# Attention on one core: the product of probabilities and values as three rounded products, one item later

## The reference, cut to what matters

```python
def one_block(qi):
    s = jnp.einsum('bqhd,bkhd->bhqk', qi, k).astype(jnp.float32) * sm_scale
    p = jax.nn.softmax(s, axis=-1).astype(v.dtype)
    return jnp.einsum('bhqk,bkhd->bqhd', p, v)
```

## Time and profile before

| | us |
|---|---|
| three runs | 4581.32, 4586.82, 4589.06 |
| median | 4586.82 |
| span of the profiled execution | 4584.7 |
| first layer's attention, items (from 583.6 us) | 7 heads at about 56.3 each, then the last |
| second layer's attention, items (from 1557.0 us) | 7 heads at about 53.1 each, then the last |

### The profile page before, as it was taken

One profiled execution on the slowest core, in us unless ns is written; L12 is line 12 of the kernel. 1 busy time (PEld: TensorE's weight loads), 2 busy tenths in 40 slices (PEclk: granted clock), 3 DMA queues, 4 the chain that ended last, 5 costly groups with the idle time before them and its releaser, 6 DMA issues. The chain is left out here.

```text
span 4584.7 us, 42478 instructions
## 1 busy us (share of the span) xinstructions
PE 3953.7 (86%) x16276; PEld 2819.4 (61%) x16276; DVE 2099.5 (46%) x2655; ACT 1550.5 (34%) x2451; POOL 673.8 (15%) x332
## 2 busy tenths in 40 slices
PE   4799799999798799996857899889999855999996
PEld 1687455568586355583636666567777744666664
DVE  0391466651372566622356423233442213666665
ACT  1412345550422445413141335222220012555542
POOL 0221200002221100020101010123333222011111
PEclk9899899999899799987988899999999966999997
DMA  4211100111210121222312110233333234999975
GB/s 165 74 37 30 35 19 29 32 42 65 78 47 26 42 66 56 65 83 53 40 40 52 45 21 10 42 75 83 88 86 68 74 112 129 359 352 358 353 290 213
DMA packets 346632, 451.05 MB, mean 98 GB/s; under 512 B 51965, under 2 KB 221106, under 8 KB 344898
## 3 DMA queue, kind: packets, MB, share of 16 engines
q1 hardware_dynamic: 331186, 405.28, 29.3%
q0 software_dynamic: 12656, 25.26, 1.5%
q10 hardware_dynamic: 2592, 17.83, 1.0%
HBM read 408.39 MB, written 59.31 MB: 102 GB/s over the span
## 5 line engine op out<-in xcount | busy, mean ns | idle before, releaser
L1144 PE MATMUL values<-probs,vp 128*128 128x512 f32 x672 | 348.6, 600 | 12.0 <-issue 6.4
L1232 ACT ACTIVATE probs<-scores 128x512 f32<-128x512 f32 (+1 forms) x336 | 196.0, 583 | 306.3 <-PE scores L219 304.6
L217 PE MATMUL scores<-q_hi,k_rest 97*128 97x512 f32 (+1 forms) x336 | 262.3, 781 | 0.0
L3382 PE MATMUL dp<-h_t,abt 128*128 128x512 f32 x544 | 241.9, 598 | 1.1 <-ACT abt L3431 0.9
L261 POOL TENSOR_TENSOR ring_r<-ring_w,ring_hi 128x1024 fp32r<-128x1024 f32 x44 | 136.8, 3111 | 702.5 <-ACT ring_hi L254 702.5
L3413 ACT ACTIVATE expert_hi<-wu 128x1024 fp32r<-128x1024 f32 x136 | 144.8, 1065 | 251.4 <-PE gp L219 251.4
L1313 DVE TENSOR_REDUCE mx<-made 128x1 f32<-128x640 f32 (+1 forms) x272 | 203.9, 794 | 27.2 <-PE made L1085 26.4
L217 PE MATMUL smb<-x_t_r,merge_w_r 128*128 128x512 f32 x480 | 196.1, 408 | 22.2 <-POOL merge_w_r L2723 19.4
L217 PE MATMUL gates_ps<-x_t_r,ring_r 128*128 128x512 f32 (+1 forms) x560 | 206.5, 369 | 2.5 <-PEq L83 2.5
L734 DVE SCALAR_TENSOR_TENSOR conv_out<-conv_in,vectors,conv_out 128x1295 f32<-128x1295 f32 (+1 forms) x120 | 205.9, 1716 | 4.3
L218 PE MATMUL gates_ps<-h_t_r,ring_hi 128*128 128x512 f32 (+1 forms) x560 | 206.4, 369 | 0.0
(11 more groups left out here) (527 smaller groups left out, 9504.9 us busy)
## 6 DMA issues: line engine op xcount, KB each, us to landing
wg<-in_w_gate SPq DMA_DIRECT2D x34, 2048.0 KB, 9.8
wu<-in_w_up SPq DMA_DIRECT2D x34, 2048.0 KB, 11.0
h_t<-in_w_down SPq DMA_DIRECT2D x34, 2048.0 KB, 9.9
ahead_w<-in_w_ada SPq DMA_DIRECT2D x48, 512.0 KB, 3.9
ring_w<-in_w_in SPq DMA_DIRECT2D x44, 512.0 KB, 4.0
mod_w<-in_w_mod ACTq DMA_DIRECT2D x8, 1536.0 KB, 29.1
ahead_w<-in_w_mod SPq DMA_DIRECT2D x24, 512.0 KB, 3.5
out_w<-in_w_out SPq DMA_DIRECT2D x24, 512.0 KB, 5.2
```

What stands on the lines that cost most here:

```text
L217: nc.tensor.matmul(out, lhs[1], rhs[0], start=start, stop=False, **kw)
L1144: nc.tensor.matmul(O[b % 2][:, 0:w], vp[g // 2 % 2][:, kb, g % 2 * VD:g % 2 * VD + P], pr[m % 3][:, 0:w], start=kb == 0, stop=kb == nk - 1 ...
L1232: nc.scalar.activation(pr[m % 3][:, 0:w], S[m % 2][:, 0:w], ACT.Exp, scale=scale).then_inc(s.exped, 1)
L3382: m = nc.tensor.matmul(dp[half][:, :], at[:, j, :], wd[u][:, j, half * 512:(half + 1) * 512], start=j == 0, stop=j == FK - 1)
```

## The change

- The value product becomes a split product of three: values and probabilities are each split into a rounded part and a rest (`v_hi`, `v_rest`; `probs_hi`, `probs_rest`).
- The probabilities of an item are rounded by ScalarE, except for the items of steps `first_k + 1` to `NB + 1` (steps 3 to 7 in the first layer, 3 to 6 in the second), which VectorE rounds. In step n it is item n+1 that is rounded, ahead of everything else in the step. GpSimd subtracts to get the rest, 336 times.
- The value product of an item is issued one step later than before.
- Value tiles: the even head's values have one place, the odd head's two; VectorE makes their rests, three instructions for two heads.
- The row of maxima and the identity in `turn_max` are float32 instead of the rounded format.
- Smaller: three tiles (`o`, `turned`, `krope`) are given up and others used in their place; the transfers for `add_ahead` have one buffer instead of two, and the six steps are others (6, 10, 13, 17, 19, 21 in place of 9, 11, 13, 17, 19, 21 in the first layer; 5, 9, 12, 15, 17, 19 in place of 8, 10, 12, 15, 17, 19 in the second). GpSimd sets constants in two instructions over all value tiles, with a tensor as input, where it had four memsets.

```diff
--- before.py
+++ after.py
@@ -956,7 +956,12 @@
...
-    ahead_slots = (first_piece + 1, first_piece + 3, first_piece + 5, NI - 5, NI - 3, NI - 1)
+    ahead_slots = (first_piece - 2, first_piece + 2, first_piece + 5, NI - 5, NI - 3, NI - 1)
+    total = NI * HEADS
+    by_act = [not first_k + 1 <= (m - 1) % NI <= NB + 1 for m in range(total)]
+    rounded_before = [sum(by_act[:m]) for m in range(total)]
@@ -977,37 +982,52 @@
...
+    pr_rest = [at_x(f"probs_rest{i}", 512, 32 * D + 2 * D * i, F32R) for i in range(3)]
+    pr_hi = [at_x(f"probs_hi{i}", 512, 28 * D + 2 * D * i, F32R) for i in (0, 1, 5)]
...
-        vp = [sb(f"vp{i}", [P, NT, 3 * VD]) for i in range(2)]
+        vh, vr = (sb(n, [P, NT, 5, VD], F32R) for n in ("v_hi", "v_rest"))
...
-        mx_r, ident_r = sb("mx_r", [P, NT], F32R), sb("ident_r", [P, P], F32R)
+        mx_r = sb("mx_r", [P, NT])
...
+        def item(m):
+            qb, kb = items[m % NI]
+            t0, w, nk = q_blocks[qb]
+            return m // NI, qb, kb, t0, w, nk
+
+        def wait_rounded(eng, m):
+            if by_act[m]:
+                eng.wait_ge(s.p_hi_act, rounded_before[m] + 1)
+            else:
+                eng.wait_ge(s.p_hi_dve, m - rounded_before[m] + 1)
@@ -1037,8 +1057,14 @@
...
-            for i in range(2):
-                once(nc.gpsimd.memset(vp[i][:, :, VD:2 * VD], 1.0))
+            ones = k.ones[:, 0:2 * VD].rearrange("p (a d) -> p a d", d=VD).unsqueeze(1).broadcast_to([P, NT, 2, VD])
+            for values, constant in ((vh, 1.0), (vr, 0.0)):
+                once(nc.gpsimd.tensor_scalar(values[:, :, 1:4:2, :], ones, constant, None, ALU.mult))
+            for m in range(total):
+                w = item(m)[4]
+                wait_rounded(pool, m)
+                nc.gpsimd.tensor_tensor(pr_rest[m % 3][:, 0:w], pr[m % 3][:, 0:w], pr_hi[m % 3][:, 0:w].bitcast(F32),
+                                        ALU.subtract).then_inc(s.p_rest, 1)
@@ -1049,7 +1075,7 @@
...
-                    pe.wait_ge(s.v_kept, 3 * ((g - 1) // 2 + 1))
+                    pe.wait_ge(s.v_rest, 3 * ((g - 1) // 2 + 1))
@@ -1088,10 +1114,8 @@
...
-                if g == 0:
-                    pe.wait_ge(s.ident_made, 1)
...
-                    m = nc.tensor.matmul(J[0:1, j // 4, (j % 4) * P:(j % 4 + 1) * P], mx_r[:, j:j + 1], ident_r[:, :],
+                    m = nc.tensor.matmul(J[0:1, j // 4, (j % 4) * P:(j % 4 + 1) * P], mx_r[:, j:j + 1], k.ident,
@@ -1132,20 +1156,24 @@
...
-            def weigh(g, n):
-                qb, kb = items[n]
-                _, w, nk = q_blocks[qb]
-                m, b = NI * g + n, NQ * g + qb
-                if n == 0:
-                    pe.wait_ge(s.v_kept, 3 * (g // 2 + 1))
+            def weigh(m):
+                g, qb, kb, _, w, nk = item(m)
+                b, e = NQ * g + qb, g % 2
+                if m % NI == 0:
+                    pe.wait_ge(s.v_rest, 3 * (g // 2 + 1))
...
-                pe.wait_ge(s.exped, m + 1)
-                nc.tensor.matmul(O[b % 2][:, 0:w], vp[g // 2 % 2][:, kb, g % 2 * VD:g % 2 * VD + P], pr[m % 3][:, 0:w],
-                                 start=kb == 0, stop=kb == nk - 1).then_inc(s.weighed, 1)
+                first = 1 + 2 * (g // 2 % 2) if e else 0
+                V, V_rest = [x[:, kb, first:first + 2, :].rearrange("p a d -> p (a d)") for x in (vh, vr)]
+                wait_rounded(pe, m)
+                nc.tensor.matmul(O[b % 2][:, 0:w], V, pr_hi[m % 3][:, 0:w], start=kb == 0, stop=False)
+                nc.tensor.matmul(O[b % 2][:, 0:w], V_rest, pr_hi[m % 3][:, 0:w], start=False, stop=False)
+                pe.wait_ge(s.p_rest, m + 1)
+                nc.tensor.matmul(O[b % 2][:, 0:w], V, pr_rest[m % 3][:, 0:w], start=False, stop=kb == nk - 1)\
+                    .then_inc(s.weighed, 1)
@@ -1156,13 +1184,15 @@
...
-                    weigh(g, n)
+                    if g or n:
+                        weigh(NI * g + n - 1)
...
+            weigh(total - 1)
@@ -1205,9 +1235,9 @@
...
-                if p >= 2:
-                    act.wait_ge(s.weighed, 2 * (p - 1) * NI)
-                dst = vp[p % 2][:, 4 * n:4 * n + m, :].rearrange("p j (a d) -> p j a d", d=VD)[:, :, 0:3:2, :]
+                if p:
+                    act.wait_ge(s.weighed, (2 * p - 1) * NI)
+                dst = of_pair(vh, p)[:, 4 * n:4 * n + m, :, :]
@@ -1231,20 +1261,26 @@
...
+            def round_weights(m):
+                w = item(m)[4]
+                act.wait_ge(s.exped, m + 1)
+                if m >= 3:
+                    act.wait_ge(s.weighed, m - 2)
+                nc.scalar.activation(pr_hi[m % 3][:, 0:w], pr[m % 3][:, 0:w], ACT.Copy).then_inc(s.p_hi_act, 1)
...
-                    act.wait_ge(s.divided, b)
+                    act.wait_ge(s.gated, b)
...
-            nc.scalar.activation(ident_r[:, :], k.ident, ACT.Copy).then_inc(s.ident_made, 1)
@@ -1252,8 +1288,12 @@
...
+            round_weights(0)
...
+                    m = NI * g + n + 1
+                    if m < total and by_act[m]:
+                        round_weights(m)
@@ -1311,6 +1351,21 @@
...
+            def rest_of_values(p, n):
+                m = min(4, NT - 4 * n)
+                dve.wait_ge(s.v_kept, 3 * p + n + 1)
+                hi_part = of_pair(vh, p)[:, 4 * n:4 * n + m, :, :].bitcast(F32)
+                dst = of_pair(vr, p)[:, 4 * n:4 * n + m, :, :]
+                src = J[:, v_banks[n], 0:m * P].rearrange("p (j a d) -> p j a d", j=m, d=VD)
+                nc.vector.tensor_tensor(dst, src, hi_part, ALU.subtract).then_inc(s.v_rest, 1)
+            def round_weights(m):
+                w = item(m)[4]
+                dve.wait_ge(s.exped, m + 1)
+                if m >= 3:
+                    dve.wait_ge(s.weighed, m - 2)
+                nc.vector.tensor_copy(pr_hi[m % 3][:, 0:w], pr[m % 3][:, 0:w]).then_inc(s.p_hi_dve, 1)
@@ -1328,16 +1383,16 @@
...
+                if g % 2 == 0 and n >= NI - 3:
+                    rest_of_values(g // 2, n - (NI - 3))
@@ -1379,6 +1434,9 @@
...
+                    m = NI * g + n + 1
+                    if m < total and not by_act[m]:
+                        round_weights(m)
...
```

55 lines of the change are left out of this document (27 added, 28 removed).

## The result

The changed kernel takes 4692.0 us in the median of 4 runs (4688.4 to 4700.0), the kernel before 4586.9 beside it (4581.3 to 4589.1). The ratio is 1.0233, with a 95% interval of 1.0219 to 1.0248. The forecast was 4644 with a range of 4568 to 4700. So the sign and the place were right, but the loss is 105 us and not 57.

A forecast was written before the change was run, and what follows sets the result against it. TensorE was taken to set the pace almost everywhere. Seven first-layer heads at 24 us, seven second-layer heads at 21 and heads 0 at 12 made +57 on 4587, so 4644 us, range 4568 to 4700.

The forecast's parts named there:

- The branch with 0.56: The forecast's main case, 4644 us, with 4620 to 4680 by two orders of arrival and the rounding's bounds; chance 0.56.
- the dear subtraction: Rival, later called the dear rival: a 512-column GpSimd subtraction takes 1.74 us, making 4692 us; chance 0.12.
- Value products: TensorE's three rounded products replace one float32: 0.16 us less per 512-column item, 3.3 per first-layer head, 3.2 per second.
- Turned maxima: Float32 turning on TensorE's own path: ten cost 1.6 us more, eight 1.3.
- GpSimd's subtraction: A 512-column subtraction on GpSimd was taken as 1.25 us, hidden in throughput below a bare item's 1.40.
- Preparation's chain: VectorE's scalings, blocked by GpSimd: 12.6 or 11.2 us for 10.0; +1.9 per first-layer head, +1.5 per second.
- First pieces: After the last scaling, the third value product comes 3.2 us later, TensorE would be there at 1.2: price 2.0 us.
- Heads of the first layer: Sum of all terms per prepared first-layer head: +3.4 us, seven heads 24.
- Heads of the second: Sum of all terms per prepared second-layer head: +3.0 us, seven heads 21.
- Last heads: Each layer's final head: 6.7 us saved by products, 4 lost to alternation and 3 at the ends, counted as 0.
- Behind the last item: Stages after attention: the prediction said nothing outside attention changes, 0 us.
- Boundaries and heads 0: Boundaries: -0.9 us per first-layer head, -0.2 per second; heads 0: constants +3.4, turning +3.0 or +2.4, both layers 12.

The follow-up runs named there:

- e1: Changed kernel without GpSimd's 336 subtractions; the third value product repeats the rounded probabilities, whose rests are left out of the result; 4607.0 us.
- e2: Changed kernel with each GpSimd subtraction replaced by three memsets of about the same total length that read nothing; the rests are zero; 4636.1 us.
- e9: Changed kernel with the edits of e1 and e4 together: no GpSimd subtractions, maxima turned in the rounded format; 4580.4 us.
- e4: Changed kernel with the maxima turned in the rounded format again, as before the change; 4659.3 us.
- e10: Changed kernel with VectorE, not GpSimd, subtracting for the items that VectorE rounds; 4697.6 us.
- e3: Changed kernel with four matmuls nobody reads ahead of the wait for the first pieces, in the second layer's heads 1 to 7; 4671.3 us.
- e6: Changed kernel with the weights for `add_ahead` loaded once per layer and never again, so the right sums are left out; 4683.0 us.
- e7: Kernel before with one edit alone: the value product, still one float32 product, comes one item later; 4574.3 us, ratio 0.9967.
- e11: Changed kernel with the edits of e10 and e4 and the matmuls of e3 in both layers; 4664.2 us.
- e12: Changed kernel with e4's edits, e3's four matmuls in the second layer, and six more in the step ahead in both layers; 4644.2 us.

## Why the forecast was right, and where its sizes were off

The sign and the mechanism were right: subtractions that hold up VectorE's rests, and a third product that waits. By the experiments the 105 us are 56 for the lock, 29 for the link and 27 for the turned maxima (e1, e2, e9), less 7 for all that is left of the change; the first two include what the lower clock behind the waits costs. That the measured time still lies in the range is in part luck. The branch with 0.56 reached to 4680 only; the upper end of 4700 covered the dear subtraction, a cause that didn't come.

*Value products, 0.16 shorter.* The bare item is 1.38 to 1.40 where 1.40 was forecast, against 1.57. What it brings over a head is smaller than the 3.3 us of the sum: steps 11 to 19 of the first layer are 1.3 us shorter, where nine items of 0.16 are 1.4, but steps 11 to 17 of the second are only 0.3 shorter, for 1.1.

*Turned maxima.* Forecast 26 us with the heads 0, measured 33 (e4) and 27 (e9 against e1). Right.

*GpSimd's subtraction.* Forecast 1.25, alone it takes 1.27 or 1.28; with its own blocked time the mean is 1.39. Right; the dear rival (1.74) was wrong, though it named the measured total.

*VectorE's rounding.* Forecast 0.49, alone it takes 0.43. The mean is 0.49 again, since 6 of the 72 are held up too, to 1.51 at most.

*Preparation's chain.* Forecast 11.2 or 12.6 us for 10.0, measured 12.25. Both orders of arrival were weighed; 21 of the 32 k rests of 512 columns are held up (19 to 1.66 or 1.67 us, two to 1.02) and 14 of the 32 q rests. The k rotations, for which a mean near 1.2 was named too, have 0.83. The Trainium skill's rule (SBUF — State Buffer, "Who interferes with whom") held with both its sides: against a GpSimd instruction that reads, 1.66 for 0.69; against one that only writes (e2), 0.69. The same section of the Trainium skill counts a VectorE copy in a 2-port mode among those that contend, too; e10's rounding of 1.49 for 0.43, which has one input in SBUF, agrees if it is such a copy.

*First pieces.* Forecast: third product 3.2 us behind the last scaling; measured 678.57 - 675.51 = 3.1. The number agrees in part by luck: the forecast took TensorE to be there at 1.2 and waiting, and in the trace it is slowed by its own clock over most of that time and its row shows no idle time ahead of that product.

*Heads of the first layer.* +3.4 forecast, +3.7 measured: the sum was right there. Of what the subtractions cost in such a head, the link is 1.6 us (e2 against e1) and the lock 2.9; in the second layer 1.9 and 2.9.

*Heads of the second.* +3.0 forecast, +5.8 measured. The step that failed is the silent one that TensorE's records keep their length: 2.1 of the missing 2.8 us per head is the fall to 1.2 GHz behind the new waits, shown by e3. The earlier trace rows have the clock at 1.00, and the forecast kept it. The other 0.7 is not accounted for.

*Last heads.* 0 forecast, +9.4 measured. `add_ahead` and the subtractions hold each other up there (4.42 and 5.72 us); with memsets (e2) these heads take 32.7 and 29.9, without GpSimd 29.0 and 26.4. The forecast counted VectorE's rounding alternating with GpSimd, not `add_ahead`.

*Behind the last item.* 0 forecast, +12. The forecast counted no transfers and said that nothing outside attention changes. Three `add_ahead` with one buffer wait some 4.0 us each for their transfers, and the next stage starts 13.7 us behind the last exponential in place of 5.2. How much of this is left at the end is not shown (e6). A later stage of the same instructions, `scan_and_merge`, takes 516.0 us in place of 507.1, from VectorE's first instruction to its last; it is 511.0 to 519.7 in all traces of changed kernels and 506.8 in e7. These two are 17 us and more than the whole, so that other stages give some back. The cause of the longer stage was not tried and stays open.

*Boundaries and heads 0.* The wait for the division is gone (steps 0 to 5: -1.4 us). Made alone (e7), the later product saves 1.1 us per head of the first layer and 0.2 of the second, where 0.9 and 0.2 were forecast. Ahead of the first item +5.9, forecast 6.4; but 2.2 of it lie ahead of attention's first matmul (519.9 us for 517.7), and from there to the first item it is 69.5 us for 65.9. So head 0 costs 3.6 us, and the agreement of the totals is chance. The turning is longer as forecast (4.43 us for 1.23).

## To carry to other kernels

An idle engine is not free help: before giving GpSimd work that reads SBUF, count the instructions of VectorE beside it that read two tiles there, and ask what releases GpSimd and what VectorE is about to do at that moment. A wait added to TensorE can cost again by the clock that falls behind it (2 us per head here in one layer, nothing that could be seen in the other), so look at the granted clock by stretches of some microseconds, not over the span. And take a bundle apart: one edit in it, the product one item later, gives the fastest of all kernels tried when it is made alone, by 0.3% against the kernel before.

## What the runs showed of the hardware beyond expectation

- GpSimd's memsets of 512 columns (0.53 us) leave VectorE's two-input instructions at 0.69 and 1.28; subtractions of the same total length make them 1.29 and 1.48 on the mean.
- The hold-up goes both ways: three subtractions of 1.28 took 5.72 us while VectorE had two `add_ahead`.
- TensorE's granted clock fell from 1.00 to 0.54 after a stretch of 4 us in which it was busy for 2.34. 28 matmuls that nobody reads, in its waits, brought the second layer's heads from 58.5 to 56.4 us and their clock from 0.93 to 0.98 (e3). With the waits of e10 the same matmuls brought it only to 0.94 (e11). In the first layer a clock of 0.99 for 0.96 brought nothing (e12 against e4).
